# Which expert blocks of a two-layer network wait in the two homes outside the weight ring

## The chip, the cores and the metric

One core of one Trainium2 chip runs the whole program. The metric is the device time of one execution, in microseconds (us). TensorE does the matmuls, VectorE (DVE), ScalarE (ACT) and GpSimd (POOL) the elementwise work, and SyncE (SP) issues every DMA, in program order, on one queue that is spread over 16 DMA engines. SBUF is the memory on the chip that weights are loaded into.

## The reference

Three transformer blocks in a row, over 256 tokens of width 1024, in float32. The first is a mixer of retention and mLSTM scans with a dense feed-forward. The second and third ("layer 0" and "layer 1" below) are an attention mixer each, followed by a mixture of 16 experts. Layer 0 also carries 256 context tokens, layer 1 the 256 tokens alone.

```python
def expert_choice_ffn(h, w_router, w1, w3, w2):      # cap = 32 tokens of 256 for each expert
    aff = softmax(h @ w_router)
    gate, idx = top_k(aff.T, cap)                     # each expert chooses its tokens
    xs = h[idx]
    a, b = xs @ w1, xs @ w3                           # each 1024 x 1024
    y = (silu(a) * b) @ w2 * gate                     # 1024 x 1024
    return zeros.at[idx].add(y)
```

An expert has three matrices of 4 MB, so a layer's experts are 192 MB that are read once and used for 32 or 64 rows. `x = x + g * expert_choice_ffn(...)` ends each of the two layers.

## The kernel before, in words

**Blocks.** All weights are cut into blocks of up to 2 MB (128 partitions by 4096 float32), in the order in which TensorE wants them. An expert has six: two halves of `w1`, two of `w3`, two of `w2`. Block `x0_7` is block 7 of layer 0's 96, that is half 1 of the first matrix of expert 1; `x1_7` is the same of layer 1.

**The ring.** `ring` has `SLOTS` = 7 places. Blocks take them in turn, and SP loads a block when the one that held its place is done with (`release`). For an expert block the old holder is done when the semaphore `experts_pe` has counted it: TensorE raises it once behind each half (and once behind the transposes of each expert). `before[name]` is the old holder of a block's place.

**The homes outside the ring.** The dictionary `beside` names the blocks that don't go through the ring. Place `SLOTS` is columns 4096 to 8191 of `arena`, free between the end of the attention and the gathering of tokens for the later experts. Place `SLOTS + 1`, in layer 1 alone, is `cT` and half of `hT`. Each home is used once in a layer. Before the change they hold `x0_0` in layer 0 and `x1_0`, `x1_1` in layer 1.

So ahead of layer 0's experts eight blocks can be loaded (seven in the ring, one beside), ahead of layer 1's nine. From then on a ring block `x0_k` waits until `x0_(k-7)` is done, and `x1_k` until `x1_(k-7)` is done, as seven places rotate.

**The order on SP.** The loop in `eng.sync` (lines 1468 to 1494) walks the blocks that are in the ring. Layer 0: `x0_1` to `x0_5`; then, where the next block's place is that of `eo0`, a wait for the end of attention and the load of `x0_0`; then `x0_6`, `x0_7`, `x0_8`, and so on. Layer 1: `x1_2` to `x1_6`; then behind the attention `x1_0`; then `x1_7`; then behind the last output projection `x1_1` and `x1_8`; then `x1_9`, and so on.

**TensorE in an expert** (`experts`, from line 1239): four halves at line 1272 (`w1`, `w3`), then `late_work`, which in the first four experts gathers tokens for later experts, then the wait for the gated product, transposes (line 1287), and two halves at line 1295 (`w2`). A half is 16 matmuls with 512 columns in layer 0 and 32 with 256 in layer 1.

Of the kernel before, what the change touches and what calls it, by code (L numbers as in the profile page):

```python
# [29 lines left out]
EARLY, SLOTS = 6, 7  # L30
# [280 lines left out]
def two_blocks(nc, t, widths, out):  # L311

    with ExitStack() as ctx:
# [5 lines left out]
        def flag(name):  # L319
            if name not in semaphores:  # L320
                semaphores[name] = ctx.enter_context(nc.semaphore(name))
            return semaphores[name]
# [18 lines left out]
        def carve(at, *shape):  # L341
            n = int(np.prod(shape))
            assert at + n <= 16384, (at, shape)
            v = arena[:, at:at + n]
            if len(shape) == 1:
                return v
            names = "abcd"[:len(shape)]
            return v.rearrange(f"p ({' '.join(names)}) -> p {' '.join(names)}",
                               **dict(zip(names[1:], shape[1:])))
# [124 lines left out]
        for name, width, cols in widths:  # L474
            src = t["weights"][at:at + P * cols].rearrange("(p n) -> p n", p=P) if cols else None
            blocks.append((name, cols, src))
            at += P * cols
        index = {name: i for i, (name, _, _) in enumerate(blocks)}
        place, before, landed = {}, {}, {}
        beside = {"x0_0": SLOTS, "x1_0": SLOTS, "x1_1": SLOTS + 1}  # L480
        holder, turns = [None] * SLOTS, [0] * (SLOTS + 2)
        n = 0
        for name, _, _ in blocks:
            if name in beside:
                s = beside[name]
                turns[s] += s - SLOTS
            else:
                if name == "ekv":
                    n = EARLY
                s = n % (EARLY if index[name] < index["ekv"] else SLOTS)  # L490
                n += 1
                before[name], holder[s] = holder[s], name
            place[name] = s
            turns[s] += 1
            landed[name] = 16 * turns[s]
# [32 lines left out]
        def flat(a):  # L528
            names = "abcd"[:len(a.shape) - 1]
            return a.rearrange(f"p {' '.join(names)} -> p ({' '.join(names)})") if len(names) > 1 else a  # L530
# [20 lines left out]
        def _(eng):  # L551
# [54 lines left out]
            def mod_total(g):  # L606

                eng.wait_ge(flag("mods_summed"), sum(len(m) for _, m, _ in MOD_GROUPS[:g + 1]))
                job = f"mod{g}"
                if jobs.new(job) > 1:  # L610
                    eng.wait_ge(*jobs.is_free(job))
                o = jobs.bank(job)
                for i in range(4):
                    ins = mm(o[32 * i:32 * i + 32, :], ones[:, 0:32], mod_acc[g % 2][i],  # L614
                             start=True, stop=True, skip_group_check=True)
                ins.then_inc(*jobs.fills(job))
# [811 lines left out]
        @block.sync  # L1428
        def _(eng):
            def load(name):  # L1430
                _, cols, src = blocks[index[name]]
                if name[0] == "x":
                    l, i = name[1:].split("_")
                    cols, src = 4096, t["experts"][int(l), int(i) // 6, int(i) % 6]
                s = place[name]
                if s == SLOTS + 1:
                    eng.dma_start(flat(cT[:]), src[:, 0:2048]).then_inc(arrived[s], 16)
                    eng.dma_start(flat(hT[:, 1]), src[:, 2048:4096]).then_inc(arrived[s], 16)
                elif s == SLOTS:
                    eng.dma_start(carve(4096, 4096), src).then_inc(arrived[s], 16)  # L1440
                else:
                    eng.dma_start(ring[:, s, 0:cols], src).then_inc(arrived[s], 16)

            def release(name):

                gone = before[name]
                if gone is None:
                    if place[name] == EARLY:
                        eng.wait_ge(*jobs.is_filled(f"modT{len(MOD_GROUPS) - 1}"))
                elif gone in mod_order:  # L1450
                    eng.wait_ge(flag("mods_summed"), mod_order.index(gone) + 1)
                elif gone[0] == "x":
                    l, i = gone[1:].split("_")
                    done = (1, 2, 3, 4, 6, 7)[int(i) % 6]
                    eng.wait_ge(flag("experts_pe"), XJ * (E * int(l) + int(i) // 6) + done)
                else:
                    eng.wait_ge(*jobs.is_filled(last_job[gone]))

            eng.dma_start(const[:], t["const_all"]).then_inc(flag("consts_in"), 16)
            eng.dma_start(vec[:], t["vectors"]).then_inc(flag("vectors_in"), 16)  # L1460
            eng.dma_start(flat(cT[:]), t["ctx"]).then_inc(flag("ctx_in"), 16)
            eng.dma_start(flat(xT[:]), t["x"]).then_inc(flag("x_in"), 16)
            names = [name for name, _, _ in blocks]
            for name in names[:4]:
                load(name)
            eng.dma_start(phase[:], t["const_ret"]).then_inc(flag("ret_consts_in"), 16)
            eng.dma_start(flat(mg_w), t["gates"]).then_inc(flag("gate_weights_in"), 16)
            for name in names[4:]:
                if name in beside:
                    continue  # L1470
                if before[name] == "m_up":
                    eng.wait_ge(*jobs.is_filled(last_job["m_up"]))
                    eng.dma_start(flat(cT[:]), t["ctx_2"]).then_inc(flag("ctx2_in"), 16)
                    eng.dma_start(phase[:, 0:M_END], t["const_even"]).then_inc(flag("even_consts_in"), 16)
                    eng.dma_start(e_gain, t["sgu_gain"].broadcast_to((P, 512))).then_inc(flag("gain_in"), 16)
                    eng.dma_start(flat(e_ws), t["sgu_w"]).then_inc(flag("ws_in"), 16)
                    eng.dma_start(phase[:, 1024:1024 + P * DEPTH2], t["router"]).then_inc(flag("router_in"), 16)
                if name == "x0_1":
                    eng.wait_ge(*jobs.is_filled("eu3"))
                    eng.dma_start(flat(e_bias), t["sgu_bias"].broadcast_to((P, 512))).then_inc(flag("bias_in"), 16)  # L1480
                if name == "ock":
                    eng.wait_ge(flag("att_out_even"), 1)
                    eng.dma_start(phase[:, 0:M_END], t["const_odd"]).then_inc(flag("odd_consts_in"), 16)
                if before[name] == "eo0":
                    eng.wait_ge(*jobs.is_filled("ea_o7"))
                    eng.wait_ge(*jobs.is_drained("em3"))
                    load("x0_0")
                if before[name] == "oo0":
                    eng.wait_ge(*jobs.is_filled("oa_o3"))
                    load("x1_0")  # L1490
                release(name)
                if before[name] == "oo1":
                    load("x1_1")
                load(name)
            for a in range(2):
                eng.wait_ge(flag("out_normed"), 4 * a + 4)
                eng.dma_start(out[:, 1024 * a:1024 * a + 1024],
                              flat(xT[:, 4 * a:4 * a + 4, :])).then_inc(flag("out_written"), 16)
            eng.wait_ge(flag("out_written"), 32)
# [1310 lines left out]
```

## Time and profile before

| what | value |
|---|---|
| median of 3 runs | 2028.95 us (2027.98 to 2032.73) |
| the profiled execution | 2028.93 us |
| its span | 2026.8 us |
| mean granted TensorE clock | 0.952 |
| HBM read | 580.11 MB |
| TensorE matmul busy | 1728.9 us (85%) |
| DVE, ACT, POOL busy | 646.9, 322.6, 70.6 us |

The span is that from the first to the last instruction of the profile; the execution's own time is 2.1 us longer. Times in the profile are counted from the start of the span. Layer 0's experts take about 891 to 1342 us, layer 1's mixer 1342 to 1545, layer 1's experts 1567 to 2008. A DMA is shown where SP issues it; its landing can be read from the chain of waits. "Idle before" is what an engine waited for, and "issue" there is no wait for another engine.

### The profile page before, as it was taken

The numbers are of one execution on the slowest core, as the hardware profiler recorded it, in microseconds if no ns is written. First come the engines' busy times: TensorE is split into PE (matmuls) and PEld (weight loads), VectorE is DVE, ScalarE is ACT, GpSimd is POOL, SyncE is SP. The second block draws the span as 40 slices with busy tenths as digits, with TensorE's granted clock in tenths as the row PEclk, the third lists the DMA queues.
The fourth block names the chain that finished last, engine by engine and source line by source line (L and its number), as shares of the span: only waits on it lengthen the run. The fifth ranks groups of instructions, "written<-read, shape, count | busy, mean of one in ns | idle before, by whom it ended". The sixth has DMA issues, their size and how long they took to land.

```text
span 2026.8 us, 23488 instructions
## 1 busy us (share of the span) xinstructions
PE 1728.9 (85%) x10170; PEld 1061.2 (52%) x10170; DVE 646.9 (32%) x1288; ACT 322.6 (16%) x665; POOL 70.6 (3%) x82
## 2 busy tenths in 40 slices
PE   6999999999999989989998878879998765565655
PEld 4557588888888546454433222245677432222223
DVE  2885245587842057141111111140242100000002
ACT  4101240100101135031100000021242100000001
POOL 0000321000000000000000000000140000000000
PEclk8999999999999999999999999999999988878788
DMA  9689325667625041139999999983313999999995
GB/s 402 256 327 377 125 84 197 275 276 281 249 115 228 1 162 76 60 149 400 428 428 428 427 427 427 428 378 124 123 69 141 401 428 427 427 427 427 427 428 237
DMA packets 42438, 582.67 MB, mean 287 GB/s; under 512 B 4704, under 2 KB 4960, under 8 KB 6240
## 3 DMA queue, kind: packets, MB, share of 16 engines
q1 hardware_dynamic: 42336, 581.18, 69.3%
q8 instruction: 80, 1.31, 0.3%
q14 instruction: 22, 0.18, 0.0%
HBM read 580.11 MB, written 1.05 MB: 287 GB/s over the span
## 4 chain that ended last, share of the span: by engine, by line
PE 62%; DMA 30%; DVE 5%; ACT 2%; issue 1%; SPq 0%; DVEq 0%; POOL 0%; ACTq 0%
PE banks L654 38%; DMA ring<-in_experts_dram 29%; PE banks L1272 8%; PE banks L1295 4%; PE banks L1149 3%; PE banks L954 1%; PE banks L1011 1%; DMA ring<-in_weights_dram 1%; PE banks L639 1%; PE banks L1000 1%; DVE ring L1960 1%; PE banks L1026 1%; DVE small L2402 1%; PE banks L614 0%; PE banks L626 0%
## 5 line engine op out<-in xcount | busy, mean ns | idle before, releaser
L1272 PE MATMUL banks<-ring,arena 128*32 128x256 f32 (+1 forms) x2992 | 388.6, 524 | 164.6 <-DMA ring<-in_experts_dram 164.6
L654 PE MATMUL banks<-hT,ring 128*128 128x256 f32 (+2 forms) x1728 | 405.6, 395 | 9.2 <-ACT hT L1550 8.4
L654 PEld LDWEIGHTS banks<-hT,ring 128*128 128x128 f32 (+1 forms) x1728 | 325.8, 190 | 87.8 <-issue 47.4
L1272 PEld LDWEIGHTS banks<-ring,arena 128*32 128x32 f32 (+1 forms) x2992 | 143.0, 135 | 407.9 <-DMA ring<-in_experts_dram 223.2
L1960 DVE SCALAR_TENSOR_TENSOR ring<-ring,sil_c 128x512 f32<-128x512 f32 x336 | 242.7, 750 | 7.9
L1295 PE MATMUL banks<-ring,arena 128*32 128x256 f32 (+1 forms) x1536 | 187.3, 492 | 61.2 <-DMA ring<-in_experts_dram 39.0
L2608 DVE TENSOR_TENSOR arena<-arena,banks 128x512 f32<-128x512 f32 (+1 forms) x32 | 17.7, 554 | 527.0 <-PE banks L1272 527.0
L1295 PEld LDWEIGHTS banks<-ring,arena 128*32 128x32 f32 (+1 forms) x1536 | 70.1, 127 | 161.8 <-issue 78.7
L654 PE MATMUL banks<-arena,ring 128*128 128x256 f32 (+2 forms) x720 | 151.2, 371 | 2.8 <-POOL arena L2743 1.6
L654 PE MATMUL banks<-ring,hT 128*128 128x512 f32 (+1 forms) x384 | 147.0, 541 | 2.1 <-DVE arena L2169 2.1
L654 PEld LDWEIGHTS banks<-arena,ring 128*128 128x128 f32 (+1 forms) x720 | 130.6, 188 | 23.6 <-issue 2.7
L654 PEld LDWEIGHTS banks<-ring,hT 128*128 128x128 f32 x384 | 67.7, 190 | 77.9 <-issue 74.8
L2627 DVE COPY arena<-banks 32x256 f32<-32x256 f32 (+1 forms) x36 | 18.4, 512 | 180.7 <-PE banks L1295 180.6
L654 PE MATMUL banks<-arena 128*128 128x256 f32 (+2 forms) x352 | 69.3, 345 | 3.1 <-DVE arena L2630 1.8
L654 PEld LDWEIGHTS banks<-arena 128*128 128x128 f32 x352 | 54.4, 198 | 23.0 <-issue 18.8
L654 PE MATMUL banks<-hT,arena 128*128 128x128 f32 (+1 forms) x320 | 57.6, 343 | 5.1 <-ACT hT L1542 3.0
L1849 ACT ACTIVATE arena<-banks 128x512 f32<-128x512 f32 (+1 forms) x32 | 15.7, 492 | 269.1 <-PE banks L1287 269.1
L654 PEld LDWEIGHTS banks<-hT,arena 128*128 128x128 f32 x320 | 50.9, 211 | 13.1 <-issue 9.3
L1149 PE MATMUL banks<-arena,ring 128*128 128x512 f32 x128 | 56.0, 595 | 0.0
L1842 ACT ACTIVATE arena<-banks 128x512 f32<-128x512 f32 (+1 forms) x32 | 15.7, 492 | 245.1 <-PE banks L1272 245.1
L2045 DVE SCALAR_TENSOR_TENSOR xT<-banks,mod,xT 128x256 f32<-128x256 f32 x80 | 35.0, 480 | 47.4 <-PE banks L654 47.4
L1860 ACT ACTIVATE arena<-banks 32x256 f32<-32x256 f32 (+1 forms) x36 | 16.0, 445 | 183.4 <-PE banks L1295 183.2
(324 smaller groups left out, 1229.6 us busy)
## 6 DMA issues: line engine op xcount, KB each, us to landing
ring<-in_experts_dram SPq DMA_DIRECT2D x189, 2048.0 KB, 30.5
ring<-in_weights_dram SPq DMA_DIRECT2D x73, 2048.0 KB, 12.1
ring<-in_weights_dram SPq DMA_DIRECT2D x8, 1408.0 KB, 7.9
arena<-in_experts_dram SPq DMA_DIRECT2D x2, 2048.0 KB, 8.4
ring<-in_weights_dram SPq DMA_DIRECT2D x2, 1152.0 KB, 26.5
cT<-in_ctx_dram SPq DMA_DIRECT2D x2, 1024.0 KB, 8.7
ring<-in_weights_dram SPq DMA_DIRECT2D x2, 1024.0 KB, 15.3
ring<-in_weights_dram SPq DMA_DIRECT2D x1, 1536.0 KB, 28.4
```

The source lines that it names most:

```text
L639: ins = mm(o[:, 0:N], ones, hT[:, s, k, :], start=(k == 0), stop=(k == KD - 1))
L654: ins = mm(dst, a, b, start=(i == 0), stop=(i == len(terms) - 1))
L954: ins = mm(o[64 * half:64 * half + 64, N * s:N * s + N], w[:, k, 64 * (j + 4 * half):64 * (j + 4 * half) + 64], hT[:, s, k, :], start=(k = ...
L1000: mm(jobs.bank(job)[:, 0:b.shape[-1]], a, b, start=True, stop=True).then_inc(*jobs.fills(job))
L1011: ins = mm(o[:, P * q:P * q + P], p[:, n % 2, y, P * q:P * q + P], diag[:, n % 2, y, :], start=True, stop=True)
L1026: ins = mm(o[64 * y:64 * y + 64, P * c:P * c + P], values(s, q, j, y), pT[n % 2][:, y, q, :], start=(q == 0), stop=(q == kc - 1), skip_gro ...
L1149: ins = mm(o[:, :], w[:, k, P * a:P * a + P], e_cat[:, k, :], start=(i == 0), stop=(i == 7))
L1272: ins = mm(banks[M * q:M * q + M, which, 0:W], xc[:, 4 * half + k, :], w[k][:, W * q:W * q + W], start=(half == 0 and k == 0), stop=(half ...
L1295: ins = mm(banks[M * q:M * q + M, 3, 0:W], gT[:, kk % (W // P), kk // (W // P), :], w[k][:, W * q:W * q + W], start=(kk == 0), stop=(kk == 7),
L1960: ins = STT(acc, w[:, k, :], sil_c[:, k, v:v + 1], acc, ALU.mult, ALU.add)
L2045: ins = STT(x[:, n0 + j, :], o[:, N * j:N * j + N], mod[:, L, KD * which + n0 + j, c:c + 1], x[:, n0 + j, :], ALU.mult, ALU.add)
L2402: V.tensor_reduce(a[:, y:y + 1], o[:, 0:w], AX, ALU.max).then_inc(*dve.steps())
```

## The change

The homes hold other blocks. In layer 0 `x0_7` takes the place of `x0_0`; in layer 1 `x1_7` and `x1_8` take those of `x1_0` and `x1_1`. The first blocks of a layer now go through the ring, in places that they reach one or two turns earlier. The homes are filled at the same points of SP's program as before. The load of a bias that stood ahead of `x0_1`, the first ring block, now stands ahead of `x0_0`, which is the first ring block after the change.

```diff
-        beside = {"x0_0": SLOTS, "x1_0": SLOTS, "x1_1": SLOTS + 1}
+        beside = {"x0_7": SLOTS, "x1_7": SLOTS, "x1_8": SLOTS + 1}
...
-                if name == "x0_1":
+                if name == "x0_0":
                     eng.wait_ge(*jobs.is_filled("eu3"))
                     eng.dma_start(flat(e_bias), t["sgu_bias"].broadcast_to((P, 512))).then_inc(flag("bias_in"), 16)
...
                 if before[name] == "eo0":
                     eng.wait_ge(*jobs.is_filled("ea_o7"))
                     eng.wait_ge(*jobs.is_drained("em3"))
-                    load("x0_0")
+                    load("x0_7")
                 if before[name] == "oo0":
                     eng.wait_ge(*jobs.is_filled("oa_o3"))
-                    load("x1_0")
+                    load("x1_7")
                 release(name)
                 if before[name] == "oo1":
-                    load("x1_1")
+                    load("x1_8")
                 load(name)
```

## Rows read from the trace of the kernel before

**Rows 1.** The page: span, DMA by slice, instruction queue, chain by engine.
```profile
span 2026.8 us, 23488 instructions
...
DMA  9689325667625041139999999983313999999995
...
q8 instruction: 80, 1.31, 0.3%
...
PE 62%; DMA 30%; DVE 5%; ACT 2%; issue 1%; SPq 0%; DVEq 0%; POOL 0%; ACTq 0%
```

**Rows 2.** Busy time by stretch: length, engines, granted clock, DMA share, GB/s.
```profile
1100.00:1200.00 100.00, 80.78 (x364) 27.83 (x360) 12.73 (x23) 8.29 (x14) 0.00 (x0) 1.00 1.01 427
...
1800.00:1900.00 100.00, 58.97 (x670) 27.12 (x666) 7.29 (x17) 5.31 (x14) 0.00 (x0) 0.79 1.01 427
```

**Rows 3.** The chain that ended last, around 1080 us, and where layer 0's experts end.
```profile
1080.15 30.55 DMA ring<-in_experts_dram
...
1114.44 30.55 DMA ring<-in_experts_dram
...
1297.15 30.54 DMA ring<-in_experts_dram
...
1363.87 47.41 PE banks L654 x160
```

**Rows 4.** Timeline of SP's queue: the loads ahead of layer 0's experts.
```profile
738.91 2.65 SPq L1442 DMA_DIRECT2D ring<-in_experts_dram  x5
...
865.18 0.33 SPq L1442 DMA_DIRECT2D ring<-in_experts_dram  x1
```

**Rows 5.** The same queue: x0_8, x0_9, x0_11, x0_17, x0_23, x0_29, x0_35.
```profile
897.77 0.33 SPq L1442 DMA_DIRECT2D ring<-in_experts_dram  x1
...
901.20 0.33 SPq L1442 DMA_DIRECT2D ring<-in_experts_dram  x1
...
915.86 0.33 SPq L1442 DMA_DIRECT2D ring<-in_experts_dram  x1
...
942.54 0.33 SPq L1442 DMA_DIRECT2D ring<-in_experts_dram  x1
...
972.07 0.33 SPq L1442 DMA_DIRECT2D ring<-in_experts_dram  x1
...
1001.60 0.33 SPq L1442 DMA_DIRECT2D ring<-in_experts_dram  x1
...
1025.47 0.33 SPq L1442 DMA_DIRECT2D ring<-in_experts_dram  x1
```

**Rows 6.** Timeline of TensorE in layer 0's first two experts.
```profile
890.65 3.65 PE L1272 MATMUL banks<-arena 128*64 128x512 f32 x16 [1.80 <-ACT arena L1821]
894.10 10.50 PE L1272 MATMUL banks<-ring,arena 128*64 128x512 f32 x48
...
912.17 7.09 PE L1295 MATMUL banks<-ring,arena 128*64 128x512 f32 x32 [1.66 <-ACT arena L1849]
919.09 13.90 PE L1272 MATMUL banks<-ring,arena 128*64 128x512 f32 x64
```

**Rows 7.** Busy time by stretch: DMA at the start of layer 0's stream, the next mixer's clock.
```profile
913.50:917.00 3.50, 3.50 (x20) 1.21 (x18) 0.00 (x0) 0.00 (x0) 0.00 (x0) 1.00 0.37 117
...
1341.00:1566.00 225.00, 203.10 (x994) 146.85 (x990) 74.46 (x160) 63.60 (x118) 29.93 (x28) 0.96 0.38 144
```

**Rows 8.** Timeline of SP's queue at layer 1's experts: x1_8, and later x1_9, x1_10.
```profile
1546.66 32.87 SPq L1442 DMA_DIRECT2D ring<-in_experts_dram  x4
...
1572.02 0.33 SPq L1442 DMA_DIRECT2D ring<-in_experts_dram  x1
...
1573.75 0.33 SPq L1442 DMA_DIRECT2D ring<-in_experts_dram  x1
```

**Rows 9.** Timeline of TensorE at the start of layer 1's experts.
```profile
1566.58 1.93 PE L1272 MATMUL banks<-arena 128*32 128x256 f32 x32 [1.80 <-ACT arena L1821]
...
1595.86 1.93 PE L1272 MATMUL banks<-ring,arena 128*32 128x256 f32 x32 [0.57 <-DMA ring<-in_experts_dram]
```

## The prediction

> **What bounds the kernel now.** I read the page first. The chain that ended last is 62% TensorE and 30% DMA, and the DMA slices stand at 9 in two long stretches [rows 1]. A chain with two owners must be read stage by stage, so the windows came next. In the middle of either layer's experts the DMA engines are busy throughout (share 1.01, 427 GB/s), while TensorE is busy 81 of 100 us in layer 0 and 59 of 100 in layer 1 [rows 2]. There the stream of blocks sets the time. The chain shows its pace: block after block is in flight for 30.55 us, one lands at 1080.15 + 30.55 = 1110.70 and the one seven places later at 1144.99 [rows 3], so a block takes 34.29 / 7 = 4.90 us. Between the two stages is a mixer in which the chain lies on TensorE (47.41 us in one piece [rows 3]).
>
> In such a stage the bytes are fixed. What can move is the instant from which the DMA engines never pause again; the end of the stage follows it one to one. So the third reading is of SP's queue where each layer's experts begin.
>
> **Layer 0 before.** Blocks are loaded long ahead: five rows at 738.91, one home, and the last ring block at 865.18 [rows 4]. TensorE begins at 890.65 with its first half, reads it from the home, and the next halves from the ring at the same pace [rows 6]. SP then waits for `x0_1`, as `x0_0` freed no ring place. It issues `x0_8` at 897.77 and `x0_9` at 901.20 [rows 5]: a half is 3.43 us, less than a block's 4.90, so the stream begins there without pauses. But the third of these (901.20 + 3.43 = 904.63) is followed by TensorE's gathers and its wait for the gated product; the next half only starts at 912.17 [rows 6], and `x0_11` is issued at 915.86 [rows 5]. The window 913.50 to 917.00 shows the pause: DMA share 0.37 [rows 7].
>
> To find the binding release, I take for each block the issue time less 4.90 us times its distance from `x0_8`. The block with the largest value fixes the stream. Before: `x0_8` 897.77; `x0_9` 896.30; `x0_11` 915.86 - 14.70 = **901.16**; `x0_17` 942.54 - 44.10 = 898.44; `x0_23` 972.07 - 73.50 = 898.57; `x0_29` 1001.60 - 102.90 = 898.70; `x0_35` 1025.47 - 132.30 = 893.17 [rows 5]. `x0_11` wins. These are the firsts behind each expert's wait for its product, the only candidates.
>
> **Layer 0 after.** The number of blocks ahead stays eight. What changes is which release lets the stream begin. `x0_8` now follows `x0_0` in its ring place, so it goes at 897.77 - 3.43 = 894.34; each of `x0_8` to `x0_14` is released by the block eight before it, not seven. TensorE's own times don't change there, as all eight blocks have landed. So the release at 915.86, that of block 4, now lets `x0_12` go: 915.86 - 19.60 = 896.26. On this count alone the gain is 901.16 - 896.26 = 4.90 us, one whole block.
>
> It does not all arrive. A home is used once. From `x0_15` on a block again waits for the one seven before it, at the same release as before. `x0_17`, `x0_23` and `x0_29` keep 898.44, 898.57 and 898.70, since in the first four experts TensorE, with its gathers, needs about 29.5 us for six blocks (1001.60 - 972.07 = 29.53 [rows 5]), just what the DMA engines need (6 x 4.90 = 29.40). These were 2.5 us from binding before; now `x0_29` binds. **Layer 0: 901.16 - 898.70 = 2.5 us.** The bounds are 0, if offsets between the DMA engines or the release latency eat it, and 4.9. I take the middle value, because it is the one worked out from releases that the change does not touch.
>
> **Between.** The mixer of layer 1 follows from the end of layer 0's experts, on TensorE [rows 3]. It moves by the same 2.5 us; its weights are behind the same stream and move too. Its cover for this edit is TensorE's own work.
>
> **Layer 1.** Two homes. Before, `x1_8` is issued at 1546.66 and the experts begin at 1566.58 [rows 8, 9]. `x1_9` waits for `x1_2` and goes at 1572.02, `x1_10` at 1573.75 [rows 8], 1.73 us for a half. A half takes a third of a block's time, so the very first release binds. After, `x1_9` follows `x1_0`: 1572.02 - 2 x 1.73 = 1568.56, which agrees with a first half that begins at 1566.58 [rows 9]. **Layer 1: 3.46 us.** A later limit like that of layer 0 is far away: TensorE waits for a landing as early as 1595.86 [rows 9], so there it follows the stream, not the stream it. The bounds are 1.7 (one release) and 4.5 (an issue beside it).
>
> **What is added.** No instruction, no byte, no wait. The same nine home and ring loads are issued at the same points of SP's program; only names trade. `x1_6`, wanted as seventh, is now the last to be issued, at about 1546.66 behind half of `x1_8`; three 2 MB blocks at most lie ahead of its landing (14.7 us, so by 1562 or so), and it is wanted after six halves and a product, past 1580. Cost nothing; without that cover it would cost what it is late. `x0_7` stays in the arena for seven halves where `x0_0` stayed for one. Its home is wanted next by the tokens gathered in the third expert's late work, on TensorE behind it in order. Cost nothing. A half read from the arena takes 3.65 us for 16 matmuls and one of three from the ring 10.50 / 3 = 3.50 [rows 6], the same but for the tail, so trading places doesn't change TensorE.
>
> **Sum.** 2.5 + 3.5 = 5.9 us (2.46 + 3.46). The profiled execution: 2028.93 - 5.9 = 2023.0, span 2026.8 - 5.9 = 2020.9. The profiled one is the median of the runs to 0.02 us, so the prediction is **2023.0 us**.
>
> **A page against a row.** The windows show one core drawing 427 GB/s [rows 2], and all of the above uses that pace. The Trainium skill's page "DMA: Bandwidth & Descriptors", section Specifications, gives about 358 GB/s as what HBM grants a core. By that figure, as an estimate, a block takes 5.86 us, `x0_29` recedes, the bounds become 898.3 before and 894.3 after, and the sum would be 4.0 + 3.5 = 7.5 us, 2021.4. The trace does not agree here, and the row decides.
>
> **Rivals.**
> *The whole block arrives* (2.5 + 2.4 more = 8.4 us, 2020.6). The releases of `x0_17`, `x0_23` and `x0_29` are 2.3 to 2.6 us above 896.26; if the engines ride over pauses that short, or reach them at different moments, up to the whole 4.9 stays. For it: in the row 913.50 to 917.00 the engines still moved data at 0.37 [rows 7]. Against: that pause did show.
> *The gain is used up* (0 to 3.5 us, 2025.5 to 2029.0). Instruction loads share the DMA engines (80 packets, 1.31 MB [rows 1]; 16.4 KB each, on one engine at 427 / 16 = 26.7 GB/s an estimate of 0.6 us), and a block has only landed when the last engine is done; or the mixer doesn't pass layer 0's gain on. For it: a few such packets on one engine are as much as this gain. Against: these loads occur in both kernels, over the whole span.
> *Slower*: the clock. Layer 1's mixer is bound by TensorE, and its granted clock there is 0.96 over 225 us [rows 7], that is about 18 us at the lower level, 1.2 GHz. The stage now begins 2.5 us earlier against the moments at which the clock changes. A microsecond at half clock costs half of one, so it takes 12 us more at 1.2 GHz to undo the gain, and 24 more in all to end at 0.3% slower: 2035. For it: the clock does fall there. Against: the same pauses stand before the same work, which bounds a shift to a few microseconds either way.
> *The change does nothing* goes with the second: were the stream already unbroken at 897.77, nothing could move. The row at 913.50 speaks against it.
>
> **How the numbers follow.** Forecast 0.64, whole block 0.18, used up 0.14, slower 0.04. A measurement of this kernel can tell about 0.3% (6.1 us) from no change. The forecast, 5.9 us, lies on that line: half of it counts as faster. Faster 0.32 + 0.18 = 0.50; within 0.32 + 0.14 = 0.46; slower 0.04. For the range: at the low end the whole block and the issue beside it, 2028.95 - 9.4 = 2019.5; at the high end layer 1 alone, 2025.5, and 1.3 us for a clock step or an instruction load at the wrong place, 2026.8. The likeliest case alone spans 2021.5 to 2024.5.
>
> **What would show it.** In the profile after: `x0_8` issued near 894.3; `x0_12` near 915.9; `x0_17`, `x0_23` and `x0_29` at 942.5, 972.1 and 1001.6 as before; the landings in the middle of layer 0 about 2.5 us earlier, and the mixer's 47 us piece at about 1361.4; `x1_9` issued 3.5 us earlier than the shift of the layer gives, near 1566.1; TensorE's first wait for a landing earlier in each layer; the DMA share unchanged in the middle. The prediction is wrong if the landings of layer 0 move by 0 or by 4.9, or if the mixer between takes a different time.

## The result, and the profile after

The changed kernel takes 2023.56 us in the median of 11 runs (2021.79 to 2028.05), the kernel before 2029.83 beside it (2027.58 to 2033.19). The ratio is 0.9976 with a 95% interval of 0.9967 to 0.9985: 4.9 us faster, between 3.0 and 6.7. The two medians themselves lie 6.3 us apart; single runs of one kernel scatter by about as much, so the ratio with its interval and the stages below count, not the medians. The forecast was 5.9 us. The profiled execution took 2023.56 us over a span of 2021.6.

The page of the kernel after answers to [rows 1]:
```profile
span 2021.6 us, 23488 instructions
...
DMA  9679324676635031239999999993313999999995
...
q8 instruction: 80, 1.31, 0.3%
...
PE 61%; DMA 30%; DVE 5%; ACT 2%; issue 1%; SPq 0%; DVEq 0%; POOL 0%; ACTq 0%
```
Nothing in it shows the change: the same two stretches of DMA, the same shares. The stages must be read one by one, each from its own start, because everything here happens to begin 1.38 us later (TensorE's first half at 892.03 against 890.65 [rows 6]), which the change has no part in: in the other runs below it begins between 890.04 and 893.34, with either kind of homes.

The timeline of TensorE, then that of SP's queue, at layer 0's first experts:
```profile
892.03 13.95 PE L1272 MATMUL banks<-ring,arena 128*64 128x512 f32 x64 [1.79 <-ACT arena L1821]
```
```profile
895.71 0.33 SPq L1442 DMA_DIRECT2D ring<-in_experts_dram  x1
...
917.23 0.33 SPq L1442 DMA_DIRECT2D ring<-in_experts_dram  x1
...
943.90 0.33 SPq L1442 DMA_DIRECT2D ring<-in_experts_dram  x1
...
973.42 0.33 SPq L1442 DMA_DIRECT2D ring<-in_experts_dram  x1
...
1002.94 0.33 SPq L1442 DMA_DIRECT2D ring<-in_experts_dram  x1
```
These are `x0_8`, `x0_12`, `x0_17`, `x0_23` and `x0_29`. Counted from the first half, `x0_8` goes at 3.68 us (before: 7.12 [rows 5, 6]), and the release at 25.20 lets `x0_12` go, where it let `x0_11` go. The three later ones stand at 51.87, 81.39 and 110.91, as before (51.89, 81.42, 110.95).

The windows say the same. The columns are those of [rows 2]. At 913.50 to 917.00 the DMA engines are now busy, share 0.92 for 0.37 before [rows 7]; the same stretch counted from the first half is 914.88 to 918.38 here, and its share is 0.87. The pace in mid-stage is the old one:
```profile
913.50:917.00 3.50, 3.47 (x16) 1.21 (x18) 0.00 (x0) 0.00 (x0) 0.00 (x0) 1.00 0.92 393
1100.00:1200.00 100.00, 81.91 (x370) 28.23 (x368) 12.73 (x23) 8.27 (x14) 0.00 (x0) 1.00 1.01 428
1800.00:1900.00 100.00, 57.00 (x658) 26.42 (x658) 6.44 (x15) 4.92 (x13) 0.00 (x0) 0.80 1.01 427
1341.00:1563.00 222.00, 200.07 (x990) 145.81 (x990) 73.98 (x160) 62.60 (x117) 29.92 (x28) 0.97 0.37 144
```

The chain (start and length of each link; start plus length of a DMA link is the landing), at the last wait of layer 0 for a landing (block `x0_93`), at the mixer's long piece and at the last landing of all:
```profile
1295.90 30.74 DMA ring<-in_experts_dram
...
1362.80 46.93 PE banks L654 x160
...
1418.14 7.09 PE banks L1362 x32
...
1966.90 33.03 DMA ring<-in_experts_dram
```
And the two lines of the kernel before that [rows 3] left out:
```profile
1419.69 8.55 PE banks L1362 x32
...
1973.10 32.06 DMA ring<-in_experts_dram
```
Layer 1's first half and its first streamed block, `x1_9`, in the kernel after:
```profile
1563.71 7.11 PE L1272 MATMUL banks<-ring,arena 128*32 128x256 f32 x128 [1.79 <-ACT arena L1821]
```
```profile
1565.70 0.33 SPq L1442 DMA_DIRECT2D ring<-in_experts_dram  x1
```

From these rows the span comes apart into five pieces (us):

| piece | before | after | difference |
|---|---|---|---|
| up to layer 0's first half | 890.65 | 892.03 | +1.38 |
| to the landing of `x0_93` (1327.70; 1326.64) | 437.05 | 434.61 | **-2.44** |
| to layer 1's first half | 238.88 | 237.07 | -1.81 |
| to the last landing (2005.16; 1999.92) | 438.58 | 436.21 | **-2.37** |
| to the end | 21.6 | 21.7 | 0.0 |

The sum is -5.2, the difference of the spans. The two bold pieces are the change, 4.8 us together, which is what the ratio says. The first piece and the third are not: the mixer's gain is mostly two TensorE pieces that ran at a higher granted clock (47.41 to 46.93 at a mean of 0.97 for 0.96, 8.55 to 7.09 at 1.00 for 0.83; the window over the whole mixer has 0.97 where [rows 7] has 0.96), and in the other runs below it takes 237 to 240 us with either kind of homes, except where matmuls were added to it.

### The profile page after: what moved, and what is told of

It is laid out like the page before. It is cut to its first block, busy times and chain, and to the rows that moved or that the text cites. A ratio compares the mean times of both kernels' runs of the same rounds, so it can differ in the third digit from the quotient of the medians.

```text
span 2021.6 us, 23488 instructions
## 1 busy us (share of the span) xinstructions
PE 1729.3 (86%) x10170; PEld 1061.2 (52%) x10170; DVE 646.9 (32%) x1288; ACT 321.4 (16%) x665; POOL 70.6 (3%) x82
## 3 DMA queue, kind: packets, MB, share of 16 engines
HBM read 580.11 MB, written 1.05 MB: 287 GB/s over the span
## 4 chain that ended last, share of the span: by engine, by line
PE 61%; DMA 30%; DVE 5%; ACT 2%; issue 1%; SPq 0%; DVEq 0%; POOL 0%; ACTq 0%
PE banks L654 38%; DMA ring<-in_experts_dram 29%; PE banks L1272 8%; PE banks L1295 4%; PE banks L1149 3%; PE banks L954 1%; PE banks L1011 1%; DMA ring<-in_weights_dram 1%; PE banks L639 1%; PE banks L1000 1%; DVE ring L1960 1%; PE banks L1026 1%; DVE small L2402 1%; PE banks L614 0%; PE banks L626 0%
```

## The experiments

All stage times below are counted from a layer's first half in the same kernel (line 1272 of the kernel before). "Layer 0" is the time to the landing of `x0_93`, "layer 1" that to the last landing, as in the table above.

**One layer at a time.** The homes of one layer are changed and those of the other kept; the loads on SP are renamed to match (left out here, as in the next pair).
```diff
# layer0_only
-        beside = {"x0_7": SLOTS, "x1_7": SLOTS, "x1_8": SLOTS + 1}
+        beside = {"x0_7": SLOTS, "x1_0": SLOTS, "x1_1": SLOTS + 1}
...
# layer1_only
+        beside = {"x0_0": SLOTS, "x1_7": SLOTS, "x1_8": SLOTS + 1}
...
```


> Only layer 0's home is changed (x0_7 in it, layer 1 keeps x1_0 and x1_1). Theory (the binding release): times counted from the start of layer 0's first half, x0_8 is issued 3.4 us earlier than in the kernel before and x0_12, x0_17, x0_29 at the releases of before; the last wait for a landing in layer 0 ends 2.5 us earlier; layer 1's experts gain nothing of their own. Whole kernel 2.5 us faster, ratio about 0.9988. Rival 1 (whole block): 4.9 us in layer 0. Rival 2 (start of the stream): 3.4 us, as x0_8 starts that much earlier. Rival 3 (used up): 0.

Layer 0 took 434.61, as in the changed kernel, layer 1 438.44, as before. Ratio 0.9988 (0.9975 to 1.0000).

> Only layer 1's homes are changed (x1_7 and x1_8; layer 0 keeps x0_0). Theory: layer 0 as before; counted from layer 1's first half, x1_9 is issued 3.5 us earlier and the landings follow by 3.5 us, less up to 1 us at the end, which the changed kernel lost there. Whole kernel 2.4 to 3.5 us faster, ratio 0.9983 to 0.9988. Rival (one release only counts): 1.7 us.

Layer 0 took 436.97, as before. `x1_9` was issued at 1.98 for 5.44, so 3.46 earlier, and layer 1 took 436.10: 2.5 us less. Ratio 0.9988 (0.9976 to 1.0000). The two halves of the change add up to the whole, 0.9976, and each lies in its own layer. The ratios alone would not separate 2.5 from 3.4; the stages do.

**Does the start of the stream decide, or the binding release?** In both of the next kernels `x0_8` is issued as early as in the changed one. Only the block that sits in the home differs.
```diff
# homes_3_and_12
+        beside = {"x0_3": SLOTS, "x1_1": SLOTS, "x1_2": SLOTS + 1}
...
# homes_4_and_08
+        beside = {"x0_4": SLOTS, "x1_0": SLOTS, "x1_8": SLOTS + 1}
...
```


> Other blocks in the homes: x0_3 in layer 0, x1_1 and x1_2 in layer 1. Theory: in layer 0 x0_8 starts 3.4 us earlier (released by x0_0), but x0_11 still waits for x0_4 behind the product of the first expert, 25.2 us after the first half starts, as in the kernel before; so layer 0 gains 0.0 us. Rival (start of the stream decides): 3.4 us. In layer 1 x1_9 follows x1_0, x1_10 x1_3, x1_11 x1_4: by the same count (1579.20 - 9.80 = 1569.40 against 1572.02) the gain is 2.6 us.

> Other blocks in the homes: x0_4 in layer 0, x1_0 and x1_8 in layer 1. Theory: in layer 0 x0_11 now follows x0_3 and x0_12 follows x0_5 (919.30 - 19.60 = 899.70 against 901.16): gain 1.5 us. Rival (start of the stream): 3.4; rival (a block or nothing): 4.9 or 0. In layer 1 x1_9 follows x1_1: gain 1.7 us, half of that of the changed kernel.

SP's queue with `x0_3` in the home (`x0_8`, `x0_11`), TensorE's first half, and the chain at `x0_93`:
```profile
896.26 0.33 SPq L1442 DMA_DIRECT2D ring<-in_experts_dram  x1
...
917.78 0.33 SPq L1442 DMA_DIRECT2D ring<-in_experts_dram  x1
```
```profile
892.58 7.95 PE L1272 MATMUL banks<-ring,arena 128*64 128x512 f32 x36 [1.80 <-ACT arena L1821]
```
```profile
1299.19 30.52 DMA ring<-in_experts_dram
```
The stream starts at 3.68, 3.44 us earlier than before; `x0_11` waits till 25.20 all the same, and layer 0 takes 1329.71 - 892.58 = 437.13 us, 0.1 more than before. An earlier start by itself is worth nothing.

With `x0_4` in the home, the same three readings (`x0_8`, then `x0_12` at 920.50):
```profile
895.55 0.33 SPq L1442 DMA_DIRECT2D ring<-in_experts_dram  x1
...
920.50 0.33 SPq L1442 DMA_DIRECT2D ring<-in_experts_dram  x1
```
```profile
891.87 8.38 PE L1272 MATMUL banks<-ring,arena 128*64 128x512 f32 x38 [1.80 <-ACT arena L1821]
```
```profile
1296.82 30.53 DMA ring<-in_experts_dram
```
Layer 0 takes 1327.35 - 891.87 = 435.48: 1.6 us less, where 1.5 was expected. In layer 1 of these two kernels `x1_9` went at 1.98 and 3.71, and the first of the 16 DMA engines was done with the last block 2.5 and 1.6 us earlier than before (expected 2.6 and 1.7); all 16 were done 1.4 and 2.0 us earlier. That difference is taken up below.

**What holds layer 0 at 2.5 instead of 4.9?** The forecast says the releases of `x0_17`, `x0_23` and `x0_29`, which stand behind TensorE's gathers. The first pair of kernels leaves out half of the matmuls of these gathers (in layer 0's second, third and fourth expert), with the homes of before and of after.
```diff
# half_gathers_old, half_gathers_new: in gather(), and in gather_four() for one stream
-                            sel_of[2 * s][:, c, 256 * half:256 * half + 256]) for c in range(TC)])
+                            sel_of[2 * s][:, c, 256 * half:256 * half + 256]) for c in range(TC if l else 1)])
...
-                            sel_of[2 * s][:, c, P * quarter:P * quarter + P]) for c in range(TC)])
+                            sel_of[2 * s][:, c, P * quarter:P * quarter + P]) for c in range(1 if (l, s, quarter) == (0, 1, 1) else TC)])
```


> Homes as in the kernel before. Left out: half of the matmuls of TensorE's gathers in layer 0's second, third and fourth expert (one of two token chunks; of the second expert, the context's). Theory: TensorE's gathers shrink by about 1.8, 3.6 and 3.6 us; the stream of layer 0 is still fixed by x0_11, which is released before them, so the last landing of layer 0, counted from the first half, comes as in the kernel before (0 us earlier, at most 1). Rival (TensorE's total time in layer 0 decides): about 9 us earlier.

> Homes as in the changed kernel, with the same matmuls left out as in half_gathers_old. Theory: with the gathers halved x0_23 and x0_29 no longer bind and x0_17 recedes to about 896.6, beside x0_12 at 896.26; so layer 0's last landing comes 4.5 us earlier than in half_gathers_old, where with whole gathers it was 2.5. Rival (the gain is 2.5 whatever TensorE does later): 2.5. Rival (start of the stream): 3.4.

The chain at `x0_93`, with the homes of before:
```profile
1298.27 30.52 DMA ring<-in_experts_dram
```
and with those of after:
```profile
1293.63 30.76 DMA ring<-in_experts_dram
```
Their first halves begin at 891.82 and 891.83. Layer 0 takes 436.98 with the homes of before: nearly 9 us of TensorE's work are gone (`x0_29` is issued 8.7 us earlier) and nothing is gained, since `x0_11` is released ahead of all that. With the homes of after it takes 432.56, 4.4 us less. So the gathers are what the changed kernel runs into. Ratios 0.9995 (0.9984 to 1.0005) and 0.9962 (0.9948 to 0.9976).

The second pair keeps all the work and moves part of the gathers (one, one, two and two in layer 0's first four experts) behind the expert's last half, on TensorE, ACT and DVE alike.
```diff
# split_old, split_new
+        def late_parts(l, e):
+            work = late_work(l, e)
+            if l == 1 or e >= 4:
+                return work, []
+            kept = len(work) - (1 if e < 2 else 2)
+            return work[:kept], work[kept:]
...
-                    for kind, s, *rest in late_work(l, e):
...
+                    late(0)
...
+                    late(1)
```


> Homes as in the changed kernel; all work kept, but in layer 0's first four experts part of the gathers (one, one, two, two) is done by TensorE, ACT and DVE behind the expert's last half instead of ahead of its w2 halves, so the releases of x0_17, x0_23 and x0_29 come 1.8, 3.6 and 3.6 us earlier and those of the first halves stay. Theory: the binding value falls from 898.70 to about 896.6 (x0_17) , so counted from the first half layer 0's last wait for a landing ends at 432.5 us, 4.5 earlier than in the kernel before and 2.1 earlier than in the changed kernel (434.6). Whole kernel: 2 us faster than the changed one, ratio to before about 0.9965. Rival (TensorE then waits for the gated product, or the gathers' total decides): 434.6 as in the changed kernel, or later.

> The same split of the gathers with the homes of the kernel before. Theory: layer 0's stream is still fixed by x0_11, whose release moves only by the one gather moved out of the first expert (1.8 us at most), so the last wait ends at 435.3 to 437.0 us; layer 1 as before. The moved gathers of experts two to four bring nothing. Rival (the gathers' place decides by itself): 2 to 4 us earlier.

The chain at `x0_93` in split_new, whose first half begins at 892.66:
```profile
1294.71 30.69 DMA ring<-in_experts_dram
```
Layer 0 takes 432.74, against 432.5 expected, but the agreement is luck in part. `x0_17` is issued 3.4 us earlier, not 1.8 (48.51 for 51.87 from the first half), so the releases alone would have given 5.9 us and not 4.5. Of that, 5.6 us arrive at the first of the 16 parts in which `x0_93` lands and 4.3 at the last (below). With all its work this version is the fastest: ratio 0.9963 (0.9950 to 0.9975). For comparison the changed kernel was run once more:

> The changed kernel once more, beside the kernel before. Theory: layer 0 gains 2.5 us and layer 1 at its start 3.5 us, of which the offsets between DMA engines may take about 1 by the end; the mixer between differs by 1 to 2 us either way with the clock. Ratio 0.9970 to 0.9976.

It had a ratio of 0.9980 (0.9969 to 0.9991), a little less gain than the 0.9970 to 0.9976 expected, with layer 0 434.55, layer 1 436.25. So split_new is ahead of it by the stage (1.8 us), while the two intervals overlap. split_old takes 434.96 (ratio 0.9983, 0.9974 to 0.9993), 2.1 us less than before. That is outside the expected 435.3 to 437.0 and at the lower end of the rival's range (2 to 4 us). Moving one gather out of the first expert let `x0_11` go 2.75 us earlier, not 1.8: TensorE's wait for ACT ahead of that expert's `w2` halves shrank too, from 1.66 to 0.69 us, as ACT no longer copies that gather's result ahead of it. The gain is thus that of `x0_11`'s release, by which the first part of `x0_93` lands 2.7 us earlier; by this run alone the rival isn't refuted, but half_gathers_old refutes it for the gathers of the later experts.

The count can be repeated on the issues of every kernel. For each block, issue time from the first half less 4.895 us (the mean distance of the blocks' first landings in mid-stage is 4.893 to 4.895 in both layers of both kernels) times its distance from `x0_8`; the largest value, the block that has it, and the measured time of the stage, worked out from the trace's records:
```
kernel             largest value, block   value - 10.53   layer 0, against 437.05
before             10.53  x0_11                0.0             0.0
homes_3_and_12     10.52  x0_11                0.0            +0.1
half_gathers_old   10.51  x0_11                0.0            -0.1
homes_4_and_08      9.06  x0_12               -1.5            -1.6
after               8.12  x0_29               -2.4            -2.4
layer0_only         8.12  x0_29               -2.4            -2.4
split_old           7.77  x0_11               -2.8            -2.1
half_gathers_new    6.03  x0_17               -4.5            -4.5
split_new           4.67  x0_31               -5.9            -4.3
```
In seven of the nine kernels the count gives the stage to 0.1 us; in the split pair it doesn't. There the first DMA engine's landing of `x0_93` follows (2.7 and 5.6 us earlier), and the last one's lags by 0.6 and 1.3 us more than in the kernel before. All nine have 13 instruction loads in that stage, so their number doesn't explain the lag; its cause stays open.

**Where does layer 1 lose a microsecond?** `x1_9` starts 3.46 us earlier, the stage ends only 2.37 earlier. A block has landed when the slowest of 16 DMA engines has put its part down. In the records the 16 parts of the last block land within the "spread" below. The last two columns are the instruction loads (16 KB each, on one DMA engine, queue 8) between the issue of `x1_9` and the last landing: their number, and how long after that issue the first comes. Times are from layer 1's first half:
```
kernel             x1_9 issued   first part   last part   spread   loads   first load after
before                 5.44        433.27       438.58      5.3      24        9.6
layer0_only            5.44        433.29       438.44      5.2      24       10.0
half_gathers_old       5.44        433.29       438.47      5.2      25        0.4
split_old              5.44        433.32       438.61      5.3      24        9.5
homes_4_and_08         3.71        431.63       436.61      5.0      24       11.9
homes_3_and_12         1.98        430.76       437.14      6.4      25        3.9
after                  1.98        429.81       436.21      6.4      25        3.9
after_again            1.98        429.68       436.25      6.6      25        3.9
layer1_only            1.98        429.91       436.10      6.2      25        3.7
half_gathers_new       1.98        429.70       435.98      6.3      25        6.5
split_new              1.98        429.79       436.03      6.2      25        3.5
```
In the changed kernel the first part gains the full 3.5 us; the last one doesn't. The large spread goes with a 25th load inside the stream (in half_gathers_old the first of the 25 comes before the stream's data move). The stream that starts earlier takes in a load that fell ahead of it before (3.2 us behind the first half in the kernel before, where `x1_9` goes at 5.44; 5.9 in the changed one, where it goes at 1.98). The parts can be followed from block to block. In mid-stream each load sets one part back, mostly by 1.4 to 1.7 us, and the steps go round the same eight of the 16 parts. Here are these eight at the last two blocks, as distances from the block's first part:
```
before  x1_94   3.45 4.76 4.80 4.94 4.97 4.99 5.26 5.39
before  x1_95   3.60 4.74 4.78 4.87 4.92 4.93 5.22 5.31
after   x1_94   4.30 4.52 4.76 4.79 4.91 4.95 5.05 5.15
after   x1_95   4.27 4.48 4.75 4.87 4.91 5.02 5.10 6.40
```
In either kernel a load begins 2.2 to 2.3 us ahead of the last landing (at 2002.84 and 1997.76). In the kernel before, one of the eight parts had been hit once less than the others and takes it, almost without effect. In the changed kernel, one load further on, all eight had been hit equally often, and the next load sets one of them back to 6.40. The records don't name the engine of a load; that is read from the steps. To test this, 80 tiny matmuls on TensorE ahead of layer 1's experts shift its instruction loads:
```diff
+                if l == 1:
+                    for _ in range(80):
+                        mm(banks[0:32, 3, 0:2], ones[:, 0:32], const[:, 0:2], start=True, stop=True)
```


> The changed kernel with 80 tiny matmuls on TensorE just ahead of layer 1's first expert, which shift TensorE's instruction loads by 160 instructions. Theory (offsets): in the changed kernel an instruction load fell into the first DMA burst of layer 1, so one DMA engine was hit four times by the end, the fourth during the last block, and the last landing came 6.4 us behind the first engine's instead of 5.3. With the shift the first load falls ahead of the burst: the spread at the last block is 5.0 to 5.4 us and the last landing, counted from layer 1's first half, comes at 435.1 instead of 436.2. Rival (the 1.1 us are due to the homes or the stream itself): 436.2 as before.

> The kernel before with the same 80 tiny matmuls. Theory: no instruction load enters or leaves the stream of layer 1 (24 with and without), so the last landing stays at 438.5 us behind the first half and its spread at 5.3. Rival (the pad shortens the stage by itself): 1.1 us earlier.

The last link of the chain in pad_new:
```profile
1974.81 31.74 DMA ring<-in_experts_dram
```
Its last block is in flight for 31.74 us, where that of the changed kernel took 33.03 and that of the kernel before 32.06. The spread is 5.3 (5.0 in pad_old), with 24 loads in either, as expected. The time from the first half, however, is 436.86 and 439.88, not 435.1 and 438.5: in both padded kernels `x1_9` is issued 1.7 to 1.8 us later than in the unpadded ones, which I had not foreseen. TensorE ran first halves at the lower clock, 1.2 GHz, and in pad_new the tiny matmuls too, as the window over both shows (granted clock 0.50):
```profile
1563.00:1575.00 12.00, 12.00 (x183) 9.96 (x185) 0.00 (x0) 0.00 (x0) 0.00 (x0) 0.50 0.10 20
```
Counted from that issue, the last landing comes at 433.08 us (pad_new) for 434.23 in the changed kernel, and at 432.75 (pad_old) for 433.14 in the kernel before. So with the load shifted the microsecond is there again. The padding also moved the start of the stream, though: every kernel with the large spread issues `x1_9` at 1.98, and the kernels with 24 loads at 3.71 or later. No run has the start at 1.98 with 24 loads, so the steps of the parts above, and not pad_new alone, show that it is the load. Each padded kernel was run once. The mixers of both take 245 us; as versions they are of no use.

## Why the prediction was right

**The bound.** Right. Both experts' stages end when their stream ends, and the stream ends where its binding release puts it, to within the distance between the 16 parts. homes_3_and_12 shows that an earlier start is not enough.

**Layer 0, 2.5 us.** Right to 0.1 (2.44), with the binding blocks named: `x0_11` before, `x0_29` after. The rival of the whole block, 4.9, fails in the full kernel and comes within about half a microsecond of true only when the gathers are halved (4.4) or moved (4.3).

**Between.** The mixer passes the gain on. It also differs by 1.8 us in the profiled pair, with the clock, which the forecast had as a risk to either side. It fell on the good side there; with the other runs at 237 to 240 us for either kind of homes, it isn't due to the change. Among its signs of being wrong the forecast had "if the mixer between takes a different time", and in this pair it does: the mixer varies by nearly 3 us from run to run, more than the gain of a layer, so that sign was too sharp.

**Layer 1, 3.46 us.** The step "the stage's end follows the first release one to one" failed by 1.1 us: the issue moved by 3.46 exactly, the first DMA engine's last landing by 3.46 (433.27 to 429.81), the slowest engine's by 2.37. The term was mis-sized because its sum took a block as one transfer, where it is 16 that drift apart. The forecast had the cause among its rivals (instruction loads on the DMA engines, and a block that has only landed when the last engine is done), as a part of the case in which the gain is used up. That case took place, by a fifth of the gain. The forecast's argument against, that the loads occur in both kernels, missed that one more of them falls into the earlier stream. It also estimated 0.6 us for a load, where the records have about 1.05 us and a part is set back by about 1.5.

**Added costs.** None, as forecast. TensorE reads a half from either place in the same time (3.60 us from the ring and 3.60 from the home, in layer 0's second expert) and nobody waits for `x1_6`, which landed at 1556.06, ahead of the first half: in layer 1's timeline the first wait for a landing stands at 1594.36, behind thirteen halves:
```profile
1592.22 1.91 PE L1272 MATMUL banks<-ring,arena 128*32 128x256 f32 x32
1594.36 1.93 PE L1272 MATMUL banks<-ring,arena 128*32 128x256 f32 x32 [0.23 <-DMA ring<-in_experts_dram]
```
Before it was 1595.86 [rows 9], counted from the first half 29.3 us for 30.7 now. In layer 0 the first such wait went from 190.7 to 193.2. The forecast had this sign the wrong way round ("first wait for a landing earlier in each layer"): a stream that starts earlier makes TensorE wait later.

**The sum.** 5.9 forecast, 4.8 measured in the stages (2.44 + 2.37), 4.9 by the ratio. The difference is layer 1's microsecond. The forecast held 0.3% (6.1 us) to be the least that can be told from no change; the measured 0.24% has an interval of 0.15 to 0.33%, which is clear of zero, so here less than 0.3% could be told apart. That the median, 2023.56, lies only 0.6 us from 2023.0 is luck in part: the medians are 6.3 us apart, and the stages show 4.8. By the 358 GB/s of the Trainium skill's page "DMA: Bandwidth & Descriptors", section Specifications, the sum would have been 7.5 us. The trace doesn't agree with that figure: the windows show 427 GB/s in the changed kernel too, and the ratio's interval ends at 6.7.

## What to carry to other kernels

Where a stage is bound by a stream of loads, look for the release with the largest (issue time - blocks since the start x time of a block); it sets the end (here to 0.1 us in seven of nine kernels, with a drift of the parts of up to 1.3 us on top in the others and in layer 1), and an earlier first issue, or 9 us less work behind it, gave nothing. Extra buffers that are used once should hold the last of the blocks loaded ahead, because each block in a rotating place that is consumed early lets the stream begin early; but a buffer used once lends its distance only until the rotation comes round, so check the releases behind that too. Read such small effects stage by stage from each stage's own start: 2.5 us were plain there, while the ratio of whole runs had an interval that reached 1.

## What the runs showed of the hardware

A block that is spread over 16 DMA engines lands in 16 parts, and in an unbroken stream their distance grows and hardly shrinks (by less than 0.4 us, from 2.31 at `x1_15` to 1.96 at `x1_21` of the changed kernel): from 0.9 us at `x1_9` of the kernel before to 5.3 us 86 blocks later. The steps in it fall at instruction loads, 16 KB each, 1.0 to 1.1 us long in mid-stream, every 7 to 26 us in layer 1. Eight of the sixteen parts move apart step by step, mostly by 1.4 to 1.7 us, the other eight stay within about 1 us. Across the pause ahead of the stream the distance is small again (1.8 us at `x1_8`, 0.9 at `x1_9` of the kernel before). Layer 0's stage ends with less of it (3.5 us) and has 13 loads where layer 1's has 24.

That the loads cause the steps is shown by the parts followed from block to block; pad_new and the counts in the table agree. That only one engine takes each load is read from the steps, which come one part at a time.

In pad_new the granted clock was 0.50 from 1563 to 1575 us, over the tiny matmuls and the first halves behind them, although TensorE's record is busy for 12.00 of the 12.00 us; in pad_old it was 0.50 from 1569.5 to 1575.5, with 6.00 of 6.00.
